# One softmax stage over head pairs instead of two stages over single heads, in a hybrid decoder block on one core

## What is computed

```python
# forgetting attention: causal softmax with a decay, c = cumsum(log_f) for each head
s = q @ k.T * D ** -0.5 + c[:, None] - c[None, :]
o_fox = softmax(where(key_pos <= query_pos, s, -inf)) @ v      # 6 heads, 2048 queries
o_fox = o_fox * silu(f_gate)
# memory attention: no mask, 256 keys
o_mem = softmax(mq @ mk.T * D ** -0.5) @ mv                    # 4 heads, 2048 queries
o_mem = o_mem * silu(m_gate)
```

## Time and profile before

| | us |
|---|---|
| median of 3 runs | 1479.8 (1478.7 to 1481.0) |
| span of the profiled execution | 1480.9 |
| TensorE busy (matmuls) | 1312.8, 89% of the span |
| VectorE busy | 665.6, 45% |
| ScalarE busy | 576.9, 39% |
| GpSimd busy | 411.6, 28% |
| DMA, mean over the span | 112 GB/s |

### The profile page before, as it was taken

One profiled execution on the slowest core, in us unless ns is written; L12 is line 12 of the kernel. 1 busy time (PEld: TensorE's weight loads), 2 busy tenths in 40 slices (PEclk: granted clock), 3 DMA queues, 4 the chain that ended last, 5 costly groups with the idle time before them and its releaser, 6 DMA issues. The chain is left out here.

```text
span 1480.9 us, 20787 instructions
## 1 busy us (share of the span) xinstructions
PE 1312.8 (89%) x6576; PEld 1053.3 (71%) x6576; DVE 665.6 (45%) x1606; ACT 576.9 (39%) x1154; POOL 411.6 (28%) x408
## 2 busy tenths in 40 slices
PE   5898989999999999938785985999899999599997
PEld 4887878888888888814453663777678687478886
DVE  4563311110000011178874763888788798432222
ACT  3563201111111000047652874777677777421010
POOL 5223420111111011044553577222322422300000
PEclk9999999999999999959876987999999999799999
DMA  5453333331222121165321543422623520355553
GB/s 201 144 164 118 111 111 113 127 120 64 70 78 78 64 78 58 49 177 166 109 85 60 165 113 84 115 93 61 156 63 94 122 59 12 98 207 198 199 174 137
DMA packets 98908, 166.45 MB, mean 112 GB/s; under 512 B 10740, under 2 KB 51444, under 8 KB 96996
## 3 DMA queue, kind: packets, MB, share of 16 engines
q1 hardware_dynamic: 96088, 156.97, 34.7%
q10 hardware_dynamic: 2560, 8.39, 1.4%
q0 software_dynamic: 192, 0.33, 0.1%
HBM read 101.36 MB, written 64.29 MB: 112 GB/s over the span
## 5 line engine op out<-in xcount | busy, mean ns | idle before, releaser
L644 PE MATMUL col_cps<-h_T,tok_slot 128*128 128x512 f32 x2112 | 481.6, 390 | 4.0 <-POOL tok_slot L600 3.9
L644 PEld LDWEIGHTS col_cps<-h_T,tok_slot 128*128 128x128 f32 x2112 | 397.9, 188 | 87.8 <-issue 4.9
L1736 PE MATMUL out_yps<-out_w,out_mix 128*128 128x512 f32 x768 | 177.7, 394 | 19.3 <-DMA out_mix<-scr_mix 16.8
L1736 PEld LDWEIGHTS out_yps<-out_w,out_mix 128*128 128x128 f32 x768 | 145.7, 190 | 51.1 <-DMA out_mix<-scr_mix 17.1
L1540 ACT ACTIVATE fox_pT<-fox_tps 128x512 fp32r<-128x512 f32 x240 | 124.8, 531 | 88.2 <-PE fox_tps L1473 85.5
L1578 DVE TENSOR_SCALAR_CACHE_REDUCE fox_prob<-fox_sps 128x512 f32<-128x512 f32 (+2 forms) x240 | 142.0, 606 | 36.6 <-PE fox_sps L1463 33.7
L1589 DVE TENSOR_TENSOR fox_pT<-fox_tps,fox_pT 128x512 fp32r<-128x512 f32 x240 | 141.6, 604 | 21.7 <-ACT fox_pT L1540 20.9
L1473 PE MATMUL fox_tps<-all_ident,fox_prob 128*128 128x128 f32 x816 | 134.6, 278 | 15.1 <-ACT fox_prob L1532 8.2
L707 DVE COPY tok_xn<-col_cps 128x512 f32<-128x512 f32 x24 | 16.6, 692 | 287.4 <-PE col_cps L644 287.4
L1486 PE MATMUL fox_ops<-fox_pT,fox_v 128*128 128x512 f32 x480 | 137.2, 376 | 0.0
L1473 PEld LDWEIGHTS fox_tps<-all_ident,fox_prob 128*128 128x128 f32 x816 | 99.9, 141 | 45.1 <-ACT fox_prob L1532 11.6
(11 more groups left out here) (189 smaller groups left out, 1760.3 us busy)
## 6 DMA issues: line engine op xcount, KB each, us to landing
scr_split<-tok_w SPq DMA_DIRECT2D x64, 256.0 KB, 2.7
out_mix<-scr_mix SPq DMA_DIRECT2D x32, 512.0 KB, 4.2
tok_xin<-in_w_cols SPq DMA_DIRECT2D x22, 512.0 KB, 3.8
tok_xin<-in_x SPq DMA_DIRECT2D x16, 512.0 KB, 3.7
scr_gates<-tok_xn SPq DMA_DIRECT2D x32, 256.0 KB, 2.3
out_x<-in_x SPq DMA_DIRECT2D x16, 512.0 KB, 6.2
out<-out_o ACTq DMA_DIRECT2D x16, 512.0 KB, 4.9
scr_fox_v<-tok_vst SPq DMA_DIRECT2D x16, 384.0 KB, 2.9
```

The costliest lines, as they stand in the source:

```text
L644: mm = nc.tensor.matmul(cps[c][:, :], w[s][a_][:, kk, :], hT[b_][:, kk, c * CH:(c + 1) * CH], start=(kk == 0 and n == 0), stop=(kk == KT - ...
L1736: mm = nc.tensor.matmul(yps[s][:, c, :], mix[s][a][:, kk, :], w[b][:, kk, c * CH:(c + 1) * CH], start=(kk == 0 and n == 0), stop=(kk == MI ...
```

## The change

The two softmax stages become one, `attention`, which runs 40 jobs: 16 for memory (2 pairs of heads, 8 groups of 256 queries), then 24 for forgetting (3 pairs, 8 groups). A job does 256 queries of both heads of a pair. All 40 are written out, with no loop.

- Scores: head 0 lies in rows 0 to 63 of the array and head 1 in rows 64 to 127, each with its own three fp32r passes into its own PSUM bank; passes of the two heads alternate.
- Decay and mask leave TensorE: VectorE adds the decay of the keys, spread over 128 partitions by a DMA, in the instruction that takes the minimum (`tensor_tensor_reduce`); on the diagonal block it adds a tile that GpSimd has made from decay and mask. The minimum runs on from piece to piece, with the one before as its start value. For memory heads the old instruction stays.
- Transposed blocks are copied once, unsplit, by ScalarE (odd blocks) or VectorE (even ones).
- Weighted sums: plain fp32 matmuls with 64 columns of v as weights; head 0 to output partitions 0 to 63, head 1 to 64 to 127. They run two blocks behind. v is stored unsplit, so its splitting in the token stage and in the memory stage goes.
- Exponentials of more than 1280 keys are made in two pieces.
- Gating is done by VectorE on 128 partitions, the split of the output by GpSimd.
- The decay row is stored once, as negative plain fp32.
- The tiles of the first pair, the memory keys and values and the queries of three jobs are loaded while GLA runs; no tile has to be filled. Pair 1 is loaded at the start of the stage, ahead of the output weights; pair 2 while pair 1 is worked on.

```diff
+FOX_PAIRS, MEM_PAIRS = FOX_H // 2, MEM_H // 2
+QG = 256
+QSLOTS = 3
+JOBS = ([(False, p, G) for p in range(MEM_PAIRS) for G in range(T // QG)]
+        + [(True, p, G) for p in range(FOX_PAIRS) for G in range(T // QG)])
...
-                nc.gpsimd.tensor_scalar(f, f, float(R), 1.0, ALU.mult, ALU.mult).then_inc(pool_rows, 1)
+                nc.gpsimd.tensor_scalar(f, f, -float(R), 1.0, ALU.mult, ALU.mult).then_inc(pool_rows, 1)
                 pool.wait_ge(pool_rows, 1)
-                nc.gpsimd.tensor_copy(parts[HI][:, :], f).then_inc(pool_rows, 1)
...
-                pool.wait_ge(rows_stored, 80)
+                pool.dma_start(scr.crow, f).then_inc(rows_stored, 16)
+                pool.wait_ge(rows_stored, 32)
...
-                for stage in next_stages:
-                    stage.first_fill(nc.vector)
...
+    def load_pair(self, sp, p):
+        s = p % 2
+        for i in (HI, LO):
+            sp.dma_start(self.k[s][i][:, :].bitcast(F32), self.scr.split[5 + p, i]).then_inc(self.pair_loaded[s], 16)
+        sp.dma_start(self.v[s][:, :, :], self.scr.fox_v[p]).then_inc(self.pair_loaded[s], 16)
+        sp.dma_start(self.c[s][:, :, :], self.scr.crow[2 * p:2 * p + 2, :].partition_broadcast(P)
+                     ).then_inc(self.pair_loaded[s], 16)
...
+    RINGP = 4
+    LAG = 2
+    PIECE = 1024
...
+    def plan(n):
+        ahead = list(score_units(n + 1)) if n + 1 < NJ else []
+        units, done, tiles_done, out = n_keys[n], 0, 0, []
+        for m in range(units):
+            upto = min(len(ahead), -(-len(ahead) * (m + 1) * 4 // (3 * units)))
+            ready = 0
+            if ahead:
+                upto_exp = upto if m + 1 == units else done
+                ready = sum(1 for t in range(2) if all(u[0] > t for u in ahead[upto_exp:]))
+            out.append(([(k, ahead[k]) for k in range(done, upto)], list(range(tiles_done, ready))))
+            done, tiles_done = upto, max(tiles_done, ready)
+        return out
...
+                    for i, (a, b) in enumerate(PASSES):
+                        for e in range(2):
+                            rows = slice(DH * e, DH * (e + 1))
+                            keys = tiles.k[p % 2][b][rows, c * CH:c * CH + w] if fox else tiles.mem_k[b][rows, p, 0:w]
+                            mm = nc.tensor.matmul(sps[k % 2][e][:, 0:w], tiles.q[n % QSLOTS][a][rows, t * P:(t + 1) * P],
+                                                  keys, start=(i == 0), stop=(i == 2))
...
+                    if m == 0:
+                        pe.wait_ge(expd, first_exp[n + 1])
+                    for t in range(1 if fox and m == 2 * G + 1 else 0, 2):
+                        for e in range(2):
+                            mm = nc.tensor.transpose(tps[k % 2][:, e, t * P:(t + 1) * P],
+                                                     prob[n % 2][:, t, e, m * P:(m + 1) * P], ident[:, :])
...
+                    for e in range(2):
+                        rows = slice(DH * e, DH * (e + 1))
+                        values = tiles.v[p % 2][:, m, rows] if fox else tiles.mem_v[:, p, m, rows]
+                        mm = nc.tensor.matmul(ops[n % 2][rows, 0, lo:QG], values, pT[k % RINGP][:, e, lo:QG],
+                                              start=(m == 0), stop=(m == n_keys[n] - 1), skip_group_check=True)
...
+                for n in range(NJ):
+                    for m, (ahead, _) in enumerate(plan(n)):
+                        transposes(n, m)
+                        for x, u in ahead:
+                            scores(n + 1, u, first_score[n + 1] + x)
+                        waiting.append((n, m))
+                        if len(waiting) > LAG:
+                            nn, mm_ = waiting.pop(0)
+                            if mm_ == 0:
+                                spread_sums(nn)
+                            weigh(nn, mm_)
...
+                                nc.vector.tensor_tensor_reduce(
+                                    pr, ps, ck, -SCALE, nmin[n % 2][:, 2 * t + e, x - 1:x] if x else 3e38,
+                                    ALU.add, ALU.min, acc).then_inc(minned, 1)
```

More of the change, by code:

```diff
@@ L533, in project_columns @@
         a = tk.raws[0:FOX_H, :]
-        parts = [both[i][0:FOX_H, 0:T] for i in (HI, LO)]
         bf = k.sb("bf", [FOX_H, 1])
@@ new lines, in _ @@
+                for k, u in enumerate(score_units(0)):
+                    scores(0, u, k)
+                waiting = []
+                for n in range(NJ):
+                    for m, (ahead, _) in enumerate(plan(n)):
[8 more added lines that the diff above has]
+                            weigh(nn, mm_)
@@ new lines, in copy @@
+                def copy(n, m):
+                    fox, p, G = JOBS[n]
+                    k = first_key[n] + m
+                    act.wait_ge(transposed, k + 1)
+                    if k >= RINGP:
+                        act.wait_ge(weighed, k - RINGP + 1)
+                    lo = P if fox and m == 2 * G + 1 else 0
+                    nc.scalar.activation(pT[k % RINGP][:, :, lo:QG], tps[k % 2][:, :, lo:QG], ACT.Copy).then_inc(copied_act, 1)
+                for t in range(2):
+                    exponentials(0, t)
@@ new lines, in _ @@
+                for k, u in enumerate(score_units(0)):
+                    minimum(0, u, k)
+                for n in range(NJ):
+                    invert(n)
+                    for m, (ahead, _) in enumerate(plan(n)):
+                        if not by_act(first_key[n] + m):
+                            copy(n, m)
+                        for x, u in ahead:
+                            minimum(n + 1, u, first_score[n + 1] + x)
+                        if n >= 1 and m == finish_at(n):
+                            finish(n - 1)
@@ L1622, in _ @@
+                finish(NJ - 1)
             @block.gpsimd
             def _(pool):
[L1624 to L1650 removed]
@@ L1651, in _, with diagonal @@
-                rounds(pool, round_)
+                def diagonal(n):
+                    fox, p, G = JOBS[n]
+                    x = sum(1 for j in JOBS[:n] if j[0])
+                    pool.wait_ge(tiles.pair_loaded[p % 2], 64 * (p // 2 + 1))
+                    if x >= 2:
+                        pool.wait_ge(minned, first_min[n - 1])
+                    nc.gpsimd.tensor_tensor(diag[n % 2][:, :, :], tiles.c[p % 2][:, :, QG * G:QG * (G + 1)],
+                                            mask[:, :, :].to_broadcast([P, 2, QG]), ALU.add).then_inc(masked, 1)
@@ L1656 @@
+                for n in range(NJ):
+                    if n + 1 < NJ and JOBS[n + 1][0]:
+                        diagonal(n + 1)
+                    if n >= 1:
+                        split(n - 1)
+                split(NJ - 1)
 class OutWeights:
```

698 lines of the change are left out of this document (293 added, 405 removed).

## The result

The changed kernel takes 1561.0 us (median of 4 runs, 1559.8 to 1566.1) beside 1480.4 us for the kernel before (1478.7 to 1482.6) on the same chip: a ratio of 1.055, 95% interval 1.053 to 1.058. It is slower, as forecast, but by 81 us where 14 were forecast, and outside the range of 1450 to 1545.

The account below looks back on a forecast made before the run. TensorE was taken as the bound, VectorE close behind. Start 806 plus 104 memory, 386 forgetting (three pairs of 116 work and 12.6 waits), 6.5 end and 193 output gave 1495.5, median 1494 us, range 1450 to 1545.

Parts of the forecast that it names:

- The start and the end: Attention stage: starts at 806 us; after it 6.5 us of last chains, then the output stage of 193.
- The wait at 191 us: TensorE's 3.88 us wait for GpSimd's splitting of the decay rows, forecast to end with one store left.
- the 14 us between the old stages: TensorE's idle time between memory and forgetting attention, with the latter's prologue; forecast to go for sure.
- Prices on TensorE: Attention: per-instruction costs at full clock, 0.15 us for each change of array shape, 116 us of work a forgetting pair.
- The rival of row halves in series: Scores: the two heads' row halves do not run together, so scores cost twice, +81 us, 1575; chance 0.10.
- The fused minimum: VectorE's add of decay and minimum in one instruction: 0.61 us for 512 columns, bounds up to twice that.
- the rival's 1.2: VectorE's fused minimum at half rate: 36 us more a pair, 39 us more waiting, 1533 in all; chance 0.08.
- The waits in the forgetting part: TensorE waiting at job starts for ScalarE's exponentials, and for copies held up by them: 12.6 us a pair.
- The clock: Granted TensorE clock in attention: 7 us more for half clock in three new memory jobs, nothing added for forgetting.
- Waits that lower the clock: Rival: clock falls with halves of the array in use and waits in every job, costing 50 us, 1545; chance 0.05.
- a memory job in which TensorE works 3.7 of 5.6 us: Memory attention: the chain through copy and exponentials sets each of 16 jobs at 5.6 us, 90 in all.
- The rival of hidden waits: Attention: interleaving hides three quarters of 38 us of exponential waits and 5 in memory, 34 in all, 1460; chance 0.22.

Follow-up runs that it names:

- e5: Changed kernel with 16 identity transposes added at each job's start, ahead of TensorE's wait for the exponentials: 1524.4 us.
- e6: Changed kernel with each exponential cut to the last 128 columns of its piece, without scale and bias (measures only, softmax mostly left out): 1460.6 us.
- e8: Changed kernel with all transposed-block copies on VectorE and the next job's scores given out over the first half of a job: 1463.9 us.
- e4: Changed kernel with TensorE taking two key blocks a turn, so changes of shape come once per two blocks: 1516.8 us.
- e10: Changed kernel with copies on VectorE, scores over a job's first half, last sums ahead of the next job's wait, two key blocks a turn: 1469.7 us.

## Why the prediction was right in direction and wrong in size

- *The start and the end* held: first score 805.1 (806, in part by luck), tail 197 (199.5). The wait at 191 us went, and so did the 14 us between the old stages.
- *Prices on TensorE* held: steps of 1.17 us (1.16), row halves side by side (six passes and a change in 0.90 us), 118 us of work a pair (116), about 0.15 us for each change of shape. The rival of row halves in series is out.
- *The fused minimum* was a little too cheap. The first piece of a row starts every 0.61 us, as I had taken it from the earlier trace rows (1002.07 to 1002.68 in the changed kernel's timeline). A piece that goes on from the minimum before it takes 0.67; far from the rival's 1.2:

```profile
1040.58 0.75 DVE L1528 CUSTOM_DVE_ANT_0 att_prob<-att_sps,atn_c,att_nmin 128x512 f32<-128x512 f32 x1 [1.48 <-PE att_sps L1405]
...
1041.25 0.74 DVE L1528 CUSTOM_DVE_ANT_0 att_prob<-att_sps,atn_c,att_nmin 128x512 f32<-128x512 f32 x1
...
1041.92 0.68 DVE L1543 COPY att_pT<-att_tps 128x512 f32<-128x512 f32 x1
```

  VectorE has 254/3 = 85 us a pair instead of 80, ScalarE 181/3 = 60, as forecast.
- *The waits in the forgetting part* were named rightly and sized too small: 16.3 us a pair instead of 12.6, which is 11 us in all. Job by job they are the waits that the sum names, each a little longer: the second pair has 2.8, 1.8, 1.7, 1.6 and 2.0 us for the exponentials (G=0 to 4; forecast 2.4, 1.6, 1.0, 1.4, 1.6) and 2.0 and 3.0 for a copy behind exponentials (G=5 and 6; forecast 1.9 and 2.7), besides 0.8 for a copy that the sum did not have.
- *The clock* is the term that failed, and the step of the prediction that was wrong: a wait was priced as its own length, and the work behind it at full speed. The sum had 7 us for it in three memory jobs, and nothing in the forgetting part; the runs give 24 in the memory part (7.3 against 5.8 us a job, e5) and about 28 in the forgetting part. Waits that lower the clock stood among the rivals, with nearly the right price (50 us) and a chance of 0.05; the other half of that rival, the halves of the array, had no part in it (e6). The argument against it was that the old memory stage had TensorE at 88% and a clock of 0.90 (over its 90 us, not 82). That is an average over another pattern. The old stage's long waits were three, at its start and for loads, and those for exponentials were short, as the kernel before shows from 812 to 902:

```profile
PE att_sps L1458 <- DMA att_v<-scr_mem_v: 7.6, 2, 5.7
PE att_sps L1458 <- PEq L787: 6.0, 1, 6.0
PE att_tps L1473 <- ACT att_prob L1532: 1.0, 3, 0.4
```

  The new order puts a wait of about 2 us into every memory job. The sum had these waits job by job, and a memory job in which TensorE works 3.7 of 5.6 us; it did not go on to ask what such a wait does to the work behind it.
- The account: memory +21 (17 of clock beyond the 7 forecast, 3 as the chain is 5.8 us and not 5.6, 1 as the query tile was waited for 3.1 us and not 2), forgetting +45 (11 waits, 28 clock, 6 work), rest -3: +63 on a forecast span of 1495.5, that is 1558. Of the 63, 45 are clock. The clock in the forgetting part is what a subtraction leaves, with e5 giving 24 or more of the 28.
- *The rival of hidden waits* said 1460 once ScalarE's waits go. e8 measures 1464, but only after the order of work is changed, and the two numbers meet partly by chance: of e8's 30 us below the forecast span, 16 lie in the memory part (88 for 104), where the rival had 5, and 8 in the forgetting part (378 for 386), where it had most of its 28. As it was written, the change loses more by its waits and the clock than it saves in the 14 us between the stages and on the other engines.

What stays open: I did not separate what in the 28 us comes from waits for exponentials and what from waits for copies. (e5 leaves the waits for copies at 17.5 us and has a clock of 0.98, but its filler also stands behind them: its own wait of 2.99 us, at 1018.92, is followed by only some 5 us at the lower level.) Nor is it measured which waits lower the clock and which do not. And the first score of profiled executions lies between 798 and 805 us although the kernels are the same up to there, so single stage lengths are good to a few us only.

## What to carry to other kernels

Where TensorE would be busy for less than all of a short job, ask two prices of its waits: that of the wait, and that of the work behind it at the lower clock. Here TensorE waited 82 us for ScalarE, and the lower clock cost some 52 more, but unevenly: nearly half of it in the short memory jobs, and nothing after waits of up to 2 us in jobs of 19 and 22 us. An average of busy time and clock over an old stage says nothing about the new pattern of waits. Before counting an engine's sum of work, look at its order: ScalarE was busy 42% of the part and still set the time, because a short copy that TensorE needs stood behind four long exponentials; giving it to an engine with short operations, and starting the exponentials earlier, took 97 us away without a change in the arithmetic. And edits that act on the same waits don't add up: test them together before crediting any of them. A cheaper TensorE is of no use where the saving turns into waiting (e4, e10).

## What the runs showed of the hardware that was not expected

- Waits of about 2 us in each memory job of 7.3 us go with a granted clock of 0.75 (842 to 925 us); with the waits filled it is 1.00 (834 to 900) and a job takes 5.8 us (e5). Waits of 1.4 us in jobs of 5.1 us go with 1.00 (e6).
- One wait of 2.99 us is followed by some 9 us at the lower level (sums and transposes 1.05 us apart instead of 0.59) in the changed kernel, and by some 5 us in e5, where filler follows it. Waits of 1.62 and 1.96 us in longer jobs are followed by none.
- Work without a use can pay: 70 us of transposes of the identity, most of it in waits, made the kernel 37 us faster (e5).
- Score matmuls on two halves of the array's rows run side by side as fully as column halves do: six passes of 512 columns in 0.90 us with the change of shape, where 1.37 would be in series.
- The fused add and minimum of 512 columns with one source in PSUM starts every 0.61 us, like a plain operation, and every 0.67 us where it starts from an earlier minimum.
